# Folded odd-frequency transforms and modulation slabs on TensorE in a two-block network

## What is computed

```python
mod_x = silu(c) @ w_mod + b_mod          # w_mod: 1024 x 6144, twelve slabs of 512 columns
mod_c = silu(c_ctx) @ w_mod + b_mod      # only slabs 0 to 3 of it are used
hx = rmsnorm(x) * (1 + sc_a) + sh_a      # needs slabs 0 to 3
hc = rmsnorm(ctx) * (1 + csc_a) + csh_a
q, k, v, hy = split(hx @ w_in)           # k and v also from hc
attn = diff_attention(rope(q), rope(k), v)
k_f = rfft(filters)                      # filters: sin layers h1..h3, then h4, times a decay
z, x1, x2 = split(short_conv(hy))
for n, gate in enumerate((x1, x2)):      # long convolution of 512 taps, both directions
    z = gate * (irfft(rfft(z, 1024) * k_f[n], 1024)[:512] + skip[n] * z)
x = x + g_a * (concat(attn, rmsnorm(z)) @ w_out)
x = x + g_f * conv_ffn(rmsnorm(x) * (1 + sc_f) + sh_f)   # slabs 4 to 11: g_a, the ffn's, g_f
```

## Time and profile before

| | |
|---|---|
| three runs | 2027.03, 2027.11, 2024.79 us (median 2027.03) |
| span of the profiled execution | 2023.3 us, first to last instruction |
| time of that execution itself | not recorded; the runs lie 1.5 to 3.8 us above the span |
| TensorE busy | 1875.4 us, 93% of the span |
| VectorE, ScalarE, pool | 1013.9, 661.0, 162.0 us |

### The profile page before, as it was taken

The page is one execution under the profiler, slowest core; times in us unless marked ns, Lnnn a source line. Parts: engine busy times, 40 slices in busy tenths (PEclk is TensorE's granted clock), DMA queues, the critical chain, the costliest instruction groups (busy, mean ns, idle before and its releaser), DMA issues.

```text
span 2023.3 us, 18405 instructions
## 1 busy us (share of the span) xinstructions
PE 1875.4 (93%) x7086; PEld 1282.2 (63%) x7086; DVE 1013.9 (50%) x1358; ACT 661.0 (33%) x1003; POOL 162.0 (8%) x120
## 2 busy tenths in 40 slices
PE   6999898889999999999799988898989899999997
PEld 2447544344477888888475544444777668888886
DVE  6833255558545442443437658568443435333443
ACT  4151133420124331332443243254433333223231
POOL 0000200000111000000101212213300010000001
PEclk9899899999999999999899999899989999999999
DMA  7221311034322223232222111110142122232231
GB/s 240 83 83 42 125 42 42 1 125 166 125 83 85 92 95 104 89 104 78 84 92 94 42 42 42 42 45 0 63 166 84 42 84 83 83 113 94 83 108 58
DMA packets 99617, 169.41 MB, mean 84 GB/s; under 512 B 2843, under 2 KB 38171, under 8 KB 99356
## 3 DMA queue, kind: packets, MB, share of 16 engines
q1 hardware_dynamic: 97292, 159.97, 22.9%
q0 software_dynamic: 2256, 8.52, 1.3%
HBM read 166.38 MB, written 2.10 MB: 83 GB/s over the span
## 4 chain that ended last, share of the span: by engine, by line
PE 82%; DVE 9%; ACT 5%; issue 2%; POOL 1%; DMA 1%; SPq 0%; DVEq 0%; ACTq 0%; POOLq 0%
PE bank L662 11%; PE bank L663 11%; PE bank L664 11%; PE bank L649 9%; PE bank L695 5%; PE bank L696 5%; PE bank L700 4%; PE bank L856 3%; PE bank L992 2%; PE bank L750 2%; PE bank L1050 2%; PE bank L866 2%; PE bank L640 2%; PE bank L811 2%; PE bank L980 1%
## 5 line engine op out<-in xcount | busy, mean ns | idle before, releaser
L649 PE MATMUL bank<-arena,weight_slots 128*128 128x512 f32 (+1 forms) x512 | 213.3, 572 | 0.0
L649 PEld LDWEIGHTS bank<-arena,weight_slots 128*128 128x128 f32 x512 | 97.3, 194 | 101.6 <-issue 100.0
L695 PE MATMUL bank<-xn_hi,weights_hi 128*128 128x512 f32 x320 | 125.7, 393 | 6.2 <-ACT xn_hi L1196 6.2
L1191 ACT ACTIVATE weights_hi<-weight_slots 128x2048 fp32r<-128x2048 f32 (+2 forms) x46 | 77.0, 1724 | 155.6 <-DMA weight_slots<-in_ffn_w_down 66.3
L2438 POOL TENSOR_TENSOR arena<-arena 128x512 f32<-128x512 f32 (+1 forms) x38 | 52.5, 1383 | 935.2 <-ACT arena L1219 932.4
L696 PE MATMUL bank<-xn_hi,weight_slots_lo 128*128 128x512 f32 x320 | 125.6, 392 | 0.0
L1180 ACT ACTIVATE arena<-bank 128x512 f32<-128x512 f32 (+2 forms) x110 | 52.7, 516 | 207.5 <-PE bank L847 63.9
L663 PE MATMUL bank<-xn_lo,weights_hi 128*128 128x512 f32 x288 | 112.1, 389 | 0.0
L662 PE MATMUL bank<-xn_hi,weights_hi 128*128 128x512 f32 x288 | 112.1, 389 | 0.0
L664 PE MATMUL bank<-xn_hi,weight_slots_lo 128*128 128x512 f32 x288 | 112.1, 389 | 0.0
L1756 DVE TENSOR_TENSOR weight_slots_lo<-weight_slots,weights_hi 128x2048 fp32r<-128x2048 f32 (+2 forms) x42 | 84.4, 2050 | 52.0 <-ACT weights_hi L1191 52.0
(11 more groups left out here) (363 smaller groups left out, 3852.6 us busy)
## 6 DMA issues: line engine op xcount, KB each, us to landing
weight_slots<-in_w_in SPq DMA_DIRECT2D x30, 1024.0 KB, 6.1
weight_slots<-in_w_mod SPq DMA_DIRECT2D x24, 1024.0 KB, 7.2
weight_slots<-in_ffn_w_up SPq DMA_DIRECT2D x22, 1024.0 KB, 6.5
weight_slots<-in_w_up SPq DMA_DIRECT2D x16, 1024.0 KB, 6.3
weight_slots<-in_w_down SPq DMA_DIRECT2D x16, 1024.0 KB, 6.1
weight_slots<-in_w_out SPq DMA_DIRECT2D x8, 1024.0 KB, 6.5
weight_slots<-in_w_xkv SPq DMA_DIRECT2D x8, 1024.0 KB, 6.2
weight_slots<-in_ffn_w_down SPq DMA_DIRECT2D x8, 768.0 KB, 5.4
```

Of the source, the lines that this page charges most:

```text
L649: ins = mm(ps[:, 0:width], w[:, k, P * m:P * m + P], rhs[:, k, 0:width], start=k == 0, stop=k == kk - 1)
L695: mm(ps[:, 0:width], wh(k, m), x2[0][:, k, 0:width], start=k == 0, stop=False)
L1191: A(high(kind, n)[:, a:b], W[:, s_, a:b], ACT.Copy).then_inc(w_hi, 1)
```

## The change

The transforms are taken at odd frequencies only (a negacyclic convolution of twice the length, of which no Nyquist term is left). *Filters:* taps are sorted by parity, each transform of a tile is the sum and difference of an even and an odd part of two products each (`KE`, `KO`); ScalarE evicts the even part, and VectorE makes the two results (`spectrum_pair`). *z:* VectorE folds each tile of 512 tokens into a symmetric and an antisymmetric half of 256 (`fold`), so a transform has two products. *y:* the two halves are made by four products of 256 columns each, and VectorE unfolds them. Six of the eight sums of complex products in each order move from VectorE to the pool (`spectrum_sums`).

*Modulation:* TensorE multiplies the slab itself, 128 x 128 of it stationary and the 2 (or 1) columns of silu(c) moving, 32 products a slab. `mod_products` is gone. Slabs 0 to 3 stand at h2, h3 and behind the two halves of h4; 4 to 7 in the attention steps 6, 10, 14 and 17; 8 to 11 in the convolutions. The slab order becomes mod 0 to 3, k, q, v, hy 0, mod 4, hy 1, mod 5, hy 2, mod 6 to 11, out.

*q product ahead of v:* q, two tiles of v, the q rotation, four tiles of v. The pool's sums of hx1 wait for the last v.

*Transfers:* the tables are 1 MB each (were 2, 2 and 2 MB, one of them loaded twice), all on SP; the first slab goes ahead of x.

```diff
-V_ORDER = [2, 3, 4, 5, 0, 1]
+V_ORDER = list(range(FFT))
...
-EARLY_MOD_AT = {"Kim_0_0": ["mod_0"], "Kim_0_3": ["mod_1"], "Kre_1_2": ["mod_2"], "Kim_1_1": ["mod_3"]}
-
-MOD_AT = {at: [f"mod_{4 + n}"] for n, at in enumerate(
-    [("Z", 0, 1), ("y", 0, 0), ("y", 0, 1), ("y", 0, 2), ("y", 0, 3), ("Z", 1, 1), ("Z", 1, 3), ("y", 1, 0)])}
+SPECTRA = [(o, c, m) for o in range(2) for c in ("re", "im") for m in range(2)]
+
+
+STEP_MOD = {6: 4, 10: 5, 14: 6, 17: 7}
+CONV_MOD = {(0, 0): 8, (0, 1): 9, (0, 3): 10, (1, 1): 11}
...
-    j += ["h1", "h2", "h3", "norm_x"]
-    j += [f"h4_{o}_{t}_{d}" for o in range(2) for t in range(NT) for d in range(2)]
-    spectra = []
+    j += ["h1", "h2", "mod_0", "h3", "mod_1", "norm_x"]
     for o in range(2):
-        spectra += [f"Kre_{o}_{m}" for m in range(HC)] + [f"Kim_{o}_{m}" for m in range(HC)] + [f"Knyq_{o}"]
-    for n in spectra:
-        j += [n] + EARLY_MOD_AT.get(n, [])
+        j += [f"h4_{o}_{t}_{d}" for t in range(NT) for d in range(2)] + [f"mod_{2 + o}"]
+    for o, c, m in SPECTRA:
+        j += [f"KE{c}_{o}_{m}", f"KO{c}_{o}_{m}"]
     j += ["norm_ctx"]
     j += [f"k_{m}" for m in range(HEADS)] + [f"kc_{m}" for m in range(HEADS)] + [f"krot_{m}" for m in range(HEADS)]
-    j += [f"v_{t}" for t in V_ORDER]
-    j += [f"q_{m}" for m in range(HEADS)] + [f"qrot_{m}" for m in range(HEADS)]
+    j += [f"q_{m}" for m in range(HEADS)]
+    j += [f"v_{t}" for t in V_ORDER[:2]] + [f"qrot_{m}" for m in range(HEADS)] + [f"v_{t}" for t in V_ORDER[2:]]
...
-            j += [f"Zre_{o}_{m}", f"Zim_{o}_{m}"] + MOD_AT.get(("Z", o, m), [])
-        for m in range(HC):
-            j += [f"y_{o}_{m}"] + MOD_AT.get(("y", o, m), [])
+            j += [f"Zre_{o}_{m}", f"Zim_{o}_{m}"]
+            if (o, m) in CONV_MOD:
+                j += [f"mod_{CONV_MOD[o, m]}"]
+        j += [f"y_{o}_{m}" for m in range(HC)]
...
-    s += [("k", 0, "kc_3"), ("v", 0, f"v_{V_ORDER[-1]}"), ("q", 0, "q_3")] + [("hy", n, f"hy_{4 * n + 3}") for n in range(3)]
-    s += [("mod", n, f"mod_{n}") for n in range(4, 12)]
+    s += [("k", 0, "kc_3"), ("q", 0, "q_3"), ("v", 0, f"v_{V_ORDER[-1]}")]
+    for n in range(3):
+        s += [("hy", n, f"hy_{4 * n + 3}"), ("mod", 4 + n, f"mod_{4 + n}")]
+    s += [("mod", n, f"mod_{n}") for n in range(7, 12)]
...
+        Kdft = tiles(0, 4)
+        Zdft = words(4, 2 * 1024).rearrange("p (t f) -> p t f", t=2)
+        Bdft = words(8, 8 * 256).rearrange("p (f t) -> p f t", f=8)
+        folded = words(12, 4 * 512).rearrange("p (c d t) -> p c d t", c=HC, d=2)
...
-        hyt = [tile(80), tile(81)]
+        hyt = [[tile(80), tile(81)], [tile(82), tile(12)]]
...
             slab("mod", 0, io["w_mod"], 0)
-            load(Adft, io["dft"].rearrange("(t p) f -> p t f", p=P), "dft")
+            load(xin, io["xT"].rearrange("(k p) t -> p k t", p=P), "x")
             slab("mod", 1, io["w_mod"], 512)
+            load(w4[0:64, :], io["hy_w4"], "w4")
+            load(delta, io["delta"].partition_broadcast(P), "delta")
+            load(Kdft, tables["dft_k"].rearrange("(t p) f -> p t f", p=P), "dft_k")
             load(lam_in, io["lam"].partition_broadcast(P).rearrange("p (a d) -> p a d", a=4), "lam")
             load(ctxT, io["ctxT"].rearrange("(k p) t -> p k t", p=P), "ctx")
             load(tiles(82, 2), io["rope"].rearrange("(a p) t -> p a t", p=P), "rope")
             for n in range(2, 4):
                 slab("mod", n, io["w_mod"], 512 * n)
             slab("k", 0, io["w_in"], 512)
+            slab("q", 0, io["w_in"], 0)
             slab("v", 0, io["w_in"], 1024)
-            slab("q", 0, io["w_in"], 0)
             for n in range(3):
                 slab("hy", n, io["w_in"], 1536 + 512 * n)
-            for n in range(4, 12):
+                if n == 0:
+                    done(sp, f"v_{V_ORDER[-1]}")
+                    load(Zdft, tables["dft_z"].rearrange("(t p) f -> p t f", p=P), "dft_z")
+                slab("mod", 4 + n, io["w_mod"], 512 * (4 + n))
+            for n in range(7, 12):
                 slab("mod", n, io["w_mod"], 512 * n)
+                if n == 7:
+                    done(sp, f"wt_{HEADS - 1}_{NT - 1}_1")
+                    load(Bdft, tables["idft_y"].rearrange("(f p) t -> p f t", p=P), "idft")
...
+                n = conditions(s)
+                if s == 0:
+                    pe.wait_ge(sem("silu_ready"), 1)
+                w = landed("mod", s)
                 ps = begin(f"mod_{s}")
-                for c in range(conditions(s)):
-                    for m in range(4):
-                        ins = mm(ps[:, 2 * m + c:2 * m + c + 1], mod_sums(s)[c][:, P * m:P * m + P], ones[:, 0:1], start=True, stop=True)
+                for m in range(4):
+                    for k in range(KD):
+                        ins = mm(ps[:, 2 * m:2 * m + n], w[:, k, P * m:P * m + P], silu[:, k, 0:n], start=k == 0, stop=k == KD - 1)
...
+                src = (Psum_f if c == "re" else Diff_f)[o]
+                f0 = (256 if c == "im" else 0) + P * m
+                for parity in range(2):
+                    ps = begin(f"K{'EO'[parity]}{c}_{o}_{m}")
+                    for t in range(2):
+                        ins = mm(ps[:], Kdft[:, 2 * parity + t, f0:f0 + P], src[:, 2 * parity + t, :], start=t == 0, stop=t == 1)
...
+                banks = [open_bank(f"zt_{o}_{t}") for t in range(NT)]
                 for c in range(HC):
-                    if o == 0:
-                        evicted(pe, f"hy_{c}")
-                    else:
-                        pe.wait_ge(sem("z_done"), c + 1)
-                for t in range(NT):
-                    ps = begin(f"zt_{o}_{t}")
-                    for c in range(HC):
-                        ins = nc.tensor.transpose(ps[:, P * c:P * c + P], u[:, c, P * t:P * t + P], ident)
-                    end(ins)
-                for t in range(NT):
-                    evicted(pe, f"zt_{o}_{t}")
-                loaded(pe, "dft_again")
+
+                    pe.wait_ge(sem("fold_done"), 2 * (HC * o + c + 1))
+                    for t, ps in enumerate(banks):
+                        d, h = divmod(t, 2)
+                        ins = nc.tensor.transpose(ps[:, P * c:P * c + P], folded[:, c, d, P * h:P * h + P], ident)
...
+                    for d in range(2):
+                        for m in range(HC):
+
+                            if m < HC - 1:
+                                pe.wait_ge(sem("y_added"), 2 * (HC - 1) * o + 2 * m + d + 1)
+                            else:
+                                pe.wait_ge(sem("y_last"), 2 * o + d + 1)
+                            f = HC * d + m
+                            ins = mm(ps[:, 256 * d:256 * d + 256], Y[:, f, P * c:P * c + P], Bdft[:, f, :], start=m == 0, stop=m == HC - 1)
...
-            def mod_products(s):
-
-                n = slabs["mod", s][0]
-                dve.wait_ge(w_landed[n % 2], 32 * (n // 2 + 1))
-                if s >= 2:
-
-                    done(dve, f"mod_{s - 2}")
-                w = W[:, n % 2, :].rearrange("p (k c) -> p k c", k=KD)
-                accs = mod_sums(s)
-                for k in range(KD):
-                    for c, acc in enumerate(accs):
-                        g = silu[:, k, c:c + 1]
-                        if k == 0:
-                            ins = V.tensor_scalar(acc, w[:, k, :], g, None, ALU.mult)
-                        else:
-                            ins = V.scalar_tensor_tensor(acc, w[:, k, :], g, acc, ALU.mult, ALU.add)
...
+            def spectrum_pair(o, c, m):
+
+                name = f"KO{c}_{o}_{m}"
+                k = (Kre if c == "re" else Kim)[o]
+                evicted(dve, f"KE{c}_{o}_{m}")
+                ps = full(dve, name)
+                if c == "re":
+                    V.tensor_tensor(k[:, 2 + m, :], k[:, m, :], ps[:], ALU.subtract)
+                else:
+                    V.tensor_tensor(k[:, 2 + m, :], ps[:], k[:, m, :], ALU.subtract)
+                free(V.tensor_tensor(k[:, m, :], k[:, m, :], ps[:], ALU.add), name)
...
+            def fold(o, c):
+
+                z = u[:, c, :]
+                if o:
+                    for t in range(NT):
+                        done(dve, f"zt_0_{t}")
+                V.tensor_tensor(folded[:, c, 0, :], z[:, 0:256], z[:, 511:255:-1], ALU.add).then_inc(sem("fold_done"), 1)
+                V.tensor_tensor(folded[:, c, 1, :], z[:, 0:256], z[:, 511:255:-1], ALU.subtract).then_inc(sem("fold_done"), 1)
...
+                    name = f"y_{o}_{c}"
+                    ps = full(dve, name)
+                    z, skip = u[:, c, :], pc("hy_skip", HC * o + c)
+                    left, right = z[:, 255::-1], z[:, 256:512]
+                    V.scalar_tensor_tensor(right, right, skip, ps[:, 0:256], ALU.mult, ALU.add)
+                    link(V.scalar_tensor_tensor(left, left, skip, ps[:, 0:256], ALU.mult, ALU.add))
+                    V.tensor_tensor(right, right, ps[:, 256:512], ALU.add)
```

(72 more changed lines are left out.)

149 lines of the change are left out of this document (53 added, 96 removed).

## The result

The changed kernel takes 2099.71 us (median of 4 runs, 2099.26 to 2104.48) against 2027.07 for the kernel before on the same chip: a ratio of 1.0367, interval 1.0353 to 1.0382. The sign was forecast, the size was not: 2099.7 lies outside the range of 2008 to 2076. The profiled execution is the slowest of the four (2104.48); its span is 2102.5 us, 79.2 more than before, where the medians differ by 72.6. So the stages read from its trace add up to some 5 us more than the median has.

A forecast was written before the change was run, and what follows sets the result against it. TensorE, 82% of the span, was taken to bound the kernel. Terms -4.5 - 1.5 + 5.6 + 13.2 + 20.6 + 3.2 - 14.1 = +22.5 us on 2027.0 gave 2049 us, range 2008 to 2076 (8 in 10).

The forecast's parts named there:

- mod_4, 5 and 6 stand in the holes before the norm sums: Attention steps 6, 10, 14: each slab starts when the transposes end and takes 10.7 us; +4.4 each, +13.2 together.
- Start: From the kernel's start to the k product: h4 25 us late, k product at 127.2 instead of 131.73; -4.5 us.
- 8 h4 6.9 + 2.55: Start: the second eight h4 products, behind mod_2, take 6.9 us plus 2.55 for the slow clock.
- Slabs in new places: Weight slots: hy 1, requested later behind mod_4, stalls TensorE 4.9 us, plus about 0.7 for the clock; +5.6 us.
- Which clock?: All slabs: whether narrow records run at full clock (7.3 us a slab) or half (14.3); 10.7 was taken.
- The clock falls inside a slab that starts fast: Each slab: 32 records at full clock, 32 at half, 10.7 us; wide work behind costs 2.55 more.
- The rival built on it, 1974: All slabs keep full clock: k product at 100.4, convolutions 90.6 us, sum -53.3, total 1974 us; chance 0.15.
- The rival of half clock throughout, 2083: Every slab runs wholly at half clock, with 3.2 us lost behind it: total 2083 us; chance 0.08.
- Convolutions: First Z to last y: Z and y products halve, four slabs are added, 114.9 us instead of 129.0; -14.1 us.
- q ahead: Input products: q rotation before the last four v hides VectorE's rope, so hy_0 starts earlier against before; -1.5 us.
- the fold: After the last head's normalisation: eight folds on VectorE, 0.41 us each at most, stand before the transposes; +3.2 us.
- The signs listed for "right": Profile: 768 modulation records above pace, clock 0.50 around slabs, h4 near 54, waits for in_w_in and in_w_mod, L1804 gone.

The follow-up runs named there:

- e2: The changed kernel with VectorE reading a slab's result before the next score maximum, in attention steps that have a slab: 2078.64 us.
- e3: e2 with slabs 4 to 6 also moved straight behind the score products, ahead of the transposes: 2069.41 us.
- e5: The edits of e1 and e3 together on the changed kernel: 1986.32 us.
- e8: The changed kernel with slab 7 moved from step 17 to behind the first Z product, slabs 8 and 9 one place later: 2092.82 us.
- e4: The changed kernel with slabs 4 to 11 summed on VectorE again, in the places and slab order of the kernel before: 2001.59 us.
- e1: The changed kernel with 128 moving columns (the same one or two repeated) in every modulation product: 2019.02 us.
- e7: The fastest kernel (wide slabs 0 to 3 on TensorE, slabs 4 to 11 on VectorE) with v ahead of q again: 1975.05 us.
- e10: e5 with slab 7 moved from step 17 into the convolutions, as in e8: 1987.77 us.
- e11: The fastest kernel with late even slabs on VectorE, odd ones as wide TensorE products, the last four earlier than in a first such sharing: 1988.83 us.

## Why the prediction was wrong, point by point

**The step that failed** is "mod_4, 5 and 6 stand in the holes before the norm sums. The transposes end at 308.2; 10.7 brings 318.8", +4.4 each. It let a slab start as soon as TensorE was idle. A slab also needs a PSUM bank, and gives one back only when VectorE reads it; I followed the weight slots through the plan, but not the bank that each job takes. For one step: the slab starts 5.0 us late, its clock has fallen by then (13.8 for 10.7, 3.1), and the next hyena product waits 3.5. With the 4.4 forecast that makes 16.0; 15.3, 19.1 and 18.0 were measured, the upper two with a slow hyena product behind. This is 39 of the 54 us missed (in the trace; by the medians 50 were missed). e2 and e3 show each wait go when its cause is taken away, and e5 that slabs at full clock can stand in these steps at about the forecast's price: the scores behind the norm sum come 4.0 us later than before in its step 6.

**Start,** forecast -4.5, measured +2.9: the clock fell inside mod_2 as forecast, but three sizes were off. "mod_2 10.7" took 12.8, "8 h4 6.9 + 2.55" took 14.0 and "mod_3 10.7" took 13.8, as the clock fell early and did not come back in between; h4 starting 2 us earlier than forecast (52.45) gave some of it back. The range given for this term, -10 to +5, held it, but the +5 was for the landing of mod_0 or the filters, and neither interfered.

**Slabs in new places:** the landing of hy 1 (5.41 for 4.9) and of slab 7 (+20.4 for +20.6) came about as forecast. Steps 0 to 5 cost 4.6 more than forecast: the product behind the stall is 2.4 slower, not 0.7, and hy_0 and hy_2 are 1.5 and 0.8 slower than before (9.30 for 7.78, 8.26 for 7.50). e8 confirms slab 7 and its price at step 17, 20.2 us.

**Which clock?** "The clock falls inside a slab that starts fast", after some 32 records, 10.7 us: measured 10.8 to 11.5 in the convolutions and 12.8 for mod_2. That 10.7 fits so well is partly luck: in e2, e3 and e8 the same narrow slabs of the convolutions took mostly 8.7 to 9.7 us, and mod_2 took 11.9 in e4 and e8. The Trainium skill ("TensorE: Matmul & The Clock Gate", Part 1) has the clock fall after idleness and names no width; by it the back-to-back slabs would have stayed fast. The rows of the slabs at 0.50 without a gap speak against that reading, and e1 decides it. The rival built on it, 1974, had the start and the convolutions of e1 (k product 100.4 for 99.93; 90.6 for 91.5 us), but e1 took 2019.0: it lacked the same bank waits as the forecast. e5, with wide slabs in usable places, took 1986.3. The rival of half clock throughout, 2083, came nearest in number, and not for its reason.

**Convolutions,** -14.1 against -10.4: the halved products did halve (3.67 for the eight records of a Z at full clock, four m for each order; a y stage 13.98 in the trace of e5), VectorE and the pool hardly held them up (one wait of 0.69 us in y_1), the reversed reads cost nothing extra (a fold takes 0.42, forecast 0.41). Of the 3.7 us, 2.3 are in Z_1, whose first products ran slow behind a pause (8.80 for 7.03). How much rests on the moment at which the clock falls e2 shows: the same stage, not edited, took 9.6 us less there.

**q ahead** and **the fold** were sized about rightly (-2.6 for -1.5, +4.0 for +3.2), but 1.5 of the 2.6 are given back in the slower hy_0. e7 has the same pattern, 2.7 at hy_0's start and 0.9 behind it.

The signs listed for "right" nearly all came: 768 records with a mean above the pace, the waits for in_w_in and in_w_mod, no L1804, h4 at 52.45. None of them looked at a PSUM bank, so they could not tell this kernel from the one forecast.

So the parts of the change differ in worth: the folds and the order of q bring 26 us (the order some 2 of them by e7), the late slabs' move costs 98 and the start 2 to 3 as they were made, and most of that is width and place, not the engine: the same products, widened and put ahead of the transposes, leave a kernel of 1986 us. The fastest found keeps them wide at the start and on VectorE later: 1972.7, 2.8% under the kernel before.

## What to carry to other kernels

Before work is put into a hole of an engine, list everything that it needs there: the engine, its weights' slot, and its output buffer, and what stands on the releasing engine ahead of the release. A buffer rotation makes a job that is inserted wait for the reader of the job eight places back, and makes the job eight places on wait for its own reader. Matrix-vector products on TensorE should be tried with their columns repeated: here that cost no time in itself, and it kept the clock wherever TensorE had not stood idle before. And a gain of a few us in a long kernel may be taken back by clock falls elsewhere (e10), or doubled by falls that come later (e2), so look where it was won, not only at the total.

## What the runs showed that I had not expected

- Fourteen us of h4 products without a gap, wide but with 64 of the 128 rows, ran at a granted clock of 0.50 to their end (72.23 to 86.2), where the spectra with 128 rows were back at 1.00 at 105, 5 us after they began. The records of mod_3 lay between; no run took them apart.
- The granted clock reads 1.00 in the first stretch of the trace, while slabs 0 and 1 take 13.81 us, the duration of 0.50. There the durations tell the clock.
- In e1 64 records with 128 moving columns take 7.31 to 7.41 us at full clock; 64 narrow ones took 8.66 us at the least (e8), with part of them at half clock, and 13.8 at half clock throughout.
- Two slabs of 2 MB requested together took 13 us to be whole (e11), their four transfers 5.2 to 11.8 us each, where a slab by itself lands some 7 us after its request.
